# An expert loop of one expert per round, with the next expert's transposes ahead of the down product and single buffers for gathered rows and results

## The chip, the core and the metric

The program runs on one core of one Trainium2 chip. Its metric is the device time of one execution in microseconds (us). The kernel before was run three times; the median counts. One more execution was recorded by the hardware profiler.

## What is computed

Two layers of a hybrid backbone over 128 context and 512 latent tokens of width 1024, all in fp32. The change touches the last part of each layer, the expert-choice mixture: each of 16 experts picks the tokens with the highest affinity to it (16 context and 64 latent ones, 80 in all), runs them through its own SwiGLU network, and adds the weighted result to the residual.

```
aff = softmax(h @ w_router)
gsel, idx = lax.top_k(aff.transpose(0, 2, 1), C)        # C = 2*T/16: 16 or 64 tokens
xs = h[idx]                                             # each expert's tokens
hid = silu(xs @ w_gate[e]) * (xs @ w_up[e])
ye = hid @ w_down[e] * gsel
y = zeros.at[idx].add(ye);   x = x + g2 * y
```

Here h is the RMS-normed residual, modulated: h = norm(x) * (1 + scale) + shift.

## The kernel before

The kernel is written by hand for the five queues of the core (PE, DVE, ACT, POOL, SP), with counting semaphores; no scheduler reorders anything. A `Signal` holds a semaphore and how often it is raised per layer, and `at(l, n)` is the value after its n-th event of layer l. Each layer is unrolled in the program; only the expert loop is a loop of the hardware (`Fori`), on PE, DVE, ACT and SP. On POOL it is unrolled.

Per expert the work is as follows.

- **Weights.** SP copies w_gate, w_up and w_down of each expert in six units of 2 MB into the six slots of `weight_ring` (L345). Units 0 to 3 are the halves of gate and up, alternating; 4 and 5 are the halves of down. A slot is loaded again as soon as PE has raised `expert_used` for its last use.
- **Gather.** POOL fetches the 80 normed rows of an expert from DRAM (`x_unit`) by an indirect DMA into `picked` (`gather`, L1386), which has two buffers.
- **Transposes.** PE transposes the 80 x 1024 rows in eight pieces into PSUM banks 6 and 7 (`picked_transposes`, L695).
- **Modulation.** DVE multiplies them by the scale and adds the shift (`modulate_picked`, L1265 and L1267) into `picked_t`, which has two buffers, too.
- **Gate and up.** PE computes both with the weights as the stationary operand (`gate_up`, L708): 64 matmuls per unit in the source, 128 in execution, since the chip runs an fp32 matmul as two. ACT takes SiLU of the gate half (L924), DVE multiplies by the up half (`gated_hidden`, L1273).
- **Down.** PE computes 80 x 1024 results into banks 4 and 5 (`down`, L722), 16 matmuls in the source and 32 in execution.
- **Result.** DVE scales by the affinity and the gate (`gated_result`, L1280) into `added` (two buffers), and POOL adds it to `x_res` in DRAM by an indirect DMA that accumulates (L1407). Before each such scatter POOL waits for the one before, since two experts may pick the same token.

The PE loop runs eight rounds of two experts. In a round the even expert's transposes come first, then its gate and up; the odd expert's transposes stand ahead of the even expert's down product. The next round begins with the branch back (L727). DVE's loop has the same two-expert form.

```
with pe.Fori(0, EXPERTS // 2) as r:
    picked_transposes(r * 2, 0, r)
    gate_up(r * 2, 0)
    picked_transposes(r * 2 + 1, 1, r)
    down(r * 2)
    gate_up(r * 2 + 1, 1)
    down(r * 2 + 1)
```

Of the kernel before, what the change touches and what calls it, by code (L numbers as in the profile page):

```python
# [67 lines left out]
def build(nc, x_prompt, x_sample, c, cache_k, cache_v, c_ctx, norm1_g, w_mod, b_mod, w_in, conv_w, conv_b,  # L68
# [9 lines left out]
    with ctx:  # L78
# [20 lines left out]
        picked = qk_flat[0:CAP, 0:2 * D].rearrange("p (b n) -> p b n", b=2)  # L99
        added = qk_flat[0:CAP, 2 * D:4 * D].rearrange("p (b n) -> p b n", b=2)  # L100
# [3 lines left out]
        picked_t = v_sb[:, D:D + 2 * KD * CAP].rearrange("p (b k n) -> p b k n", b=2, k=KD)  # L104
# [146 lines left out]
        residual_written = [signal(f"residual_written{b}", 3 - b + EXPERTS // 2, 16) for b in range(2)]  # L251
# [15 lines left out]
        gathered = [signal(f"gathered{b}", EXPERTS // 2, 16) for b in range(2)]  # L267
        picked_transposed = signal("picked_transposed", EXPERTS)
        picked_scaled = signal("picked_scaled", EXPERTS)
        picked_ready = signal("picked_ready", EXPERTS)  # L270
# [22 lines left out]
        def tokens(t):  # L293
            return slice(t * P, (t + 1) * P)
# [107 lines left out]
        def _(pe):  # L402
# [64 lines left out]
            for l in range(DEPTH):  # L467
# [224 lines left out]
                def picked_transposes(e, b, rnd):  # L692
                    pe.wait_ge(*gathered[b].at(l, rnd + 1))
                    for k in range(KD):
                        last = nc.tensor.transpose(ps[:, 6 + k // 4, (k % 4) * CAP:(k % 4 + 1) * CAP],  # L695
                                                   picked[:, b, tokens(k)], ident[0:CAP, 0:CAP])
                    last.then_inc(picked_transposed.sem, 1)

                def gate_up(e, b):
                    pe.wait_ge(*picked_ready.at(l, e + 1))  # L700
                    for i in range(4):
                        pe.wait_ge(*expert_loaded[i].at(l, e + 1))
                        w = ring[:, UNIT_SLOTS[l][i], :].rearrange("p (k n) -> p k n", k=KD)
                        for f in range(BLK):
                            for k in range(KD):
                                for c in range(2):
# [3 lines left out]
                                        picked_t[:, b, k, :], start=(k == 0), stop=(k == KD - 1))  # L710
# [16 lines left out]
                with pe.Fori(0, EXPERTS // 2) as r:  # L727
                    picked_transposes(r * 2, 0, r)
                    gate_up(r * 2, 0)
                    picked_transposes(r * 2 + 1, 1, r)  # L730
                    down(r * 2)
                    gate_up(r * 2 + 1, 1)
                    down(r * 2 + 1)
# [209 lines left out]
        def _(dve):  # L943
# [39 lines left out]
            for l in range(DEPTH):  # L983
# [275 lines left out]
                def modulate_picked(e, b):  # L1259
                    dve.wait_ge(*picked_transposed.at(l, e + 1))  # L1260
                    dst = picked_t[:, b].rearrange("p (a k) n -> p a k n", a=2)
# [15 lines left out]
                def gated_result(e, b, rnd):  # L1277
                    dve.wait_ge(*expert_used.at(l, e * 6 + 6))
                    dve.wait_ge(*residual_written[b].at(l, rnd + (3 - b)))
                    nc.vector.scalar_tensor_tensor(added[:, b, :], ps[0:CAP, 4:6, :].rearrange("p b n -> p (b n)"),  # L1280
# [3 lines left out]
                with dve.Fori(0, EXPERTS // 2) as r:  # L1284
                    modulate_picked(r * 2, 0)
                    gated_hidden(r * 2)
                    modulate_picked(r * 2 + 1, 1)
                    gated_result(r * 2, 0, r)
                    gated_hidden(r * 2 + 1)
                    gated_result(r * 2 + 1, 1, r)  # L1290
# [14 lines left out]
        def _(pool):  # L1305
# [39 lines left out]
            for l in range(DEPTH):  # L1345
# [36 lines left out]
                def gather(e):  # L1382
                    b = e % 2
                    if e >= 2:
                        pool.wait_ge(*picked_transposed.at(l, e - 1))
                    nc.gpsimd.indirect_dma_start(  # L1386
                        out=picked[:, b, :], out_offset=None, in_=x_unit,
                        in_offset=bass.IndirectOffsetOnAxis(ap=row_idx[:, e:e + 1], axis=0))\
                      .then_inc(gathered[b].sem, 16)
# [4 lines left out]
                gather(1)  # L1394
# [5 lines left out]
                pool.wait_ge(*residual_written[0].at(l, 3))  # L1400
                pool.wait_ge(*residual_written[1].at(l, 2))
                for e in range(EXPERTS):
                    b = e % 2
                    if e > 0:
# [55 lines left out]
```

## Time and profile before

| | |
|---|---|
| median of 3 runs | 2212.54 us (2212.06 to 2217.48) |
| the profiled execution | 2215.38 us |
| its span, first to last instruction | 2213.3 us |
| mean granted TensorE clock | 0.941 of full |
| instructions | 45747 |
| expert loop of layer 0 | 481 to 1114 us |
| expert loop of layer 1 | 1572 to 2184 us |

The profile is of one execution. A busy time is the sum of an engine's instructions; PE is the matmuls, PEld the weight loads, which overlap them. An idle time stands with what ended it ("releaser"); "issue" means that the engine waited for nothing that the profile shows. [...] The two loops' ends are those of their last results.

### The profile page before, as it was taken

Reading aid. Unit: us, or ns where it says so; the run is one execution under the profiler, and the core shown is the slowest. Engines: PE = TensorE matmul, PEld = TensorE weight load, DVE = VectorE, ACT = ScalarE, POOL = GpSimd, SP = SyncE. Lnnn points to the kernel's source line nnn. Section 1 sums busy time; section 2 is a strip of 40 time slices with the busy share of each in tenths; the row PEclk is TensorE's granted clock in tenths of the full one; section 3 lists DMA queues with packets and bytes.
Section 4 is the critical chain, followed back from the end, with each engine's and each line's share of the span. In section 5 each row is a group of like instructions: output and inputs, shape, how many; then the busy total and the mean of one; then the engine's idle time right before and its main releaser. Section 6 shows DMA issues by size and latency. Waiting matters only on the chain.

```text
span 2213.3 us, 45747 instructions
## 1 busy us (share of the span) xinstructions
PE 1863.8 (84%) x21107; PEld 1234.8 (56%) x21107; DVE 634.5 (29%) x1040; ACT 310.5 (14%) x616; POOL 127.5 (6%) x155
## 2 busy tenths in 40 slices
PE   4999878959888898888859996888588888898884
PEld 2555455546665665656635553654456665766662
DVE  2089484250100110011020995823300101011011
ACT  3111253210000000000021113522000000000001
POOL 2000000100000000000010000000000000000000
PEclk9999989969999999999979998989799999999997
DMA  9247500539999999999731633033599999999993
GB/s 348 81 152 252 219 14 4 190 129 363 316 344 339 326 344 334 332 333 343 277 129 42 225 133 124 1 114 149 182 340 345 346 359 350 333 349 350 342 339 106
DMA packets 219937, 536.57 MB, mean 242 GB/s; under 512 B 5905, under 2 KB 6322, under 8 KB 219730
## 3 DMA queue, kind: packets, MB, share of 16 engines
q1 hardware_dynamic: 204416, 482.37, 60.6%
q0 software_dynamic: 12128, 41.82, 6.5%
q10 hardware_dynamic: 3186, 9.12, 1.0%
q8 instruction: 191, 3.13, 0.6%
q14 instruction: 16, 0.13, 0.0%
HBM read 508.64 MB, written 24.64 MB: 241 GB/s over the span
## 4 chain that ended last, share of the span: by engine, by line
PE 80%; DVE 8%; issue 7%; DMA 3%; ACT 2%; POOL 0%; DVEq 0%; ACTq 0%; POOLq 0%
PE ps L708 28%; PE ps L722 20%; PE ps L491 13%; PE ps L621 6%; PE ps L503 3%; PE ps L435 2%; DVE neg_m L1114 2%; PE ps L578 1%; PE ps L641 1%; PE ps L444 1%; DMA weight_ring<-in_conv_w_dram 1%; DMA out_dram<-conv_tmp 1%; DVE weight_ring L1150 1%; DVE v_sb L1267 1%; PE ps L695 1%
## 5 line engine op out<-in xcount | busy, mean ns | idle before, releaser
L708 PE MATMUL ps<-v_sb,weight_ring 128*64 128x80 f32 x16384 | 629.2, 241 | 150.5 <-issue 108.4
L708 PEld LDWEIGHTS ps<-v_sb,weight_ring 128*64 128x64 f32 x16384 | 611.5, 143 | 178.5 <-issue 177.6
L722 PE MATMUL ps<-weight_ring,mix 128*80 128x512 f32 x1024 | 445.7, 593 | 0.0
L722 PEld LDWEIGHTS ps<-weight_ring,mix 128*80 128x80 f32 x1024 | 151.0, 150 | 269.5 <-issue 268.0
L491 PE MATMUL ps<-mix,weight_ring 128*128 128x128 f32 (+1 forms) x1024 | 281.1, 435 | 4.9 <-DVE mix L1014 2.7
L491 PEld LDWEIGHTS ps<-mix,weight_ring 128*128 128x128 f32 x1024 | 155.7, 191 | 139.6 <-issue 134.2
L1273 DVE TENSOR_TENSOR mix<-mix,ps 128x320 f32<-128x320 f32 x64 | 31.2, 488 | 703.1 <-PE ps L708 703.1
L1044 DVE SCALAR_TENSOR_TENSOR weight_ring<-u_gate,conv_cols,weight_ring 128x655 f32<-128x655 f32 x240 | 195.1, 892 | 0.0
L924 ACT ACTIVATE mix<-ps 128x320 f32<-128x320 f32 x64 | 28.0, 438 | 1162.8 <-PE ps L708 1162.8
L1280 DVE SCALAR_TENSOR_TENSOR qk<-ps,gsel,gate 80x1024 f32<-80x1024 f32 x32 | 41.0, 1280 | 412.0 <-PE ps L722 412.0
L621 PE MATMUL ps<-weight_ring,mix 128*128 128x512 f32 x320 | 144.6, 608 | 1.9 <-issue 1.9
L1407 POOL DMA_INDIRECT x_res<-qk,row_idx x32 | 45.9, 1435 | 1173.0 <-DVE qk L1280 1102.4
L621 PEld LDWEIGHTS ps<-weight_ring,mix 128*128 128x128 f32 x320 | 61.3, 196 | 74.1 <-issue 74.1
L503 PE MATMUL ps<-weight_ring,mix 128*128 128x512 f32 x160 | 70.5, 596 | 0.0
L846 ACT ACTIVATE weight_ring<-ps,neg_m 128x640 f32<-128x640 f32 (+1 forms) x80 | 55.8, 706 | 2.1 <-DVE neg_m L1114 2.1
L1114 DVE TENSOR_REDUCE neg_m<-ps 128x2 f32<-128x1280 f32 (+1 forms) x40 | 50.8, 1274 | 16.6 <-PE ps L553 16.2
L503 PEld LDWEIGHTS ps<-weight_ring,mix 128*128 128x128 f32 x160 | 29.8, 190 | 40.0 <-issue 40.0
L564 PE MATMUL ps<-ident,weight_ring 128*128 128x128 f32 x168 | 32.9, 300 | 20.5 <-DVE o_tok L1133 10.0
L578 PE MATMUL ps<-v_sb,weight_ring 128*128 128x128 f32 x272 | 45.2, 310 | 4.8 <-ACT weight_ring L864 4.8
L435 PE MATMUL ps<-weight_ring,cond_silu 128*32 128x512 f32 x384 | 47.9, 617 | 0.8 <-issue 0.8
L1026 DVE TENSOR_TENSOR u_gate<-u_gate,conv_tmp 128x128 f32<-128x128 f32 (+1 forms) x16 | 7.2, 489 | 135.7 <-ACT conv_tmp L797 135.7
L578 PEld LDWEIGHTS ps<-v_sb,weight_ring 128*128 128x128 f32 x272 | 37.0, 208 | 11.1 <-ACT weight_ring L864 6.4
(176 smaller groups left out, 1146.2 us busy)
## 6 DMA issues: line engine op xcount, KB each, us to landing
weight_ring<-in_w_gate_dram SPq DMA_DIRECT2D x64, 2048.0 KB, 11.0
weight_ring<-in_w_up_dram SPq DMA_DIRECT2D x64, 2048.0 KB, 10.7
weight_ring<-in_w_down_dram SPq DMA_DIRECT2D x64, 2048.0 KB, 9.7
weight_ring<-in_w_mod_dram SPq DMA_DIRECT2D x24, 2048.0 KB, 8.2
weight_ring<-in_w_in_dram SPq DMA_DIRECT2D x10, 2048.0 KB, 12.1
weight_ring<-in_w_out_dram SPq DMA_DIRECT2D x4, 2048.0 KB, 10.5
x_res<-x_tile POOLq DMA_DIRECT2D x10, 512.0 KB, 3.7
x_unit<-x_norm ACTq DMA_DIRECT2D x10, 512.0 KB, 2.6
```

What stands on the lines that cost most here:

```text
L435: last = nc.tensor.matmul(ps[c * STRIP:(c + 1) * STRIP, 6, :], cond_silu[:, k, :], w[:, k, :], start=(k < 4), stop=(k >= 4))
L491: last = nc.tensor.matmul(ps[:, 2 * (n % 3) + bank, 0:cols.stop - cols.start], w[:, k, tokens(b)], mix[:, k, cols], start=(k == 0), stop=( ...
L503: last = nc.tensor.matmul(ps[:, 2 * (n % 3), :], mix[:, k, tokens(t)], w[:, k, :], start=(k == 0), stop=(k == KD - 1))
L578: last = nc.tensor.matmul(ps[:, 7, tokens(1)], a_col[:, tokens(j)], vals, start=(j == 0), stop=(j == n - 1))
L621: last = nc.tensor.matmul(ps[:, 2 * (i % 2) + n, :], mix[:, k, tokens(t)], w[:, k % 4, n * BANK:(n + 1) * BANK], start=(k == 0), stop=(k = ...
L708: last = nc.tensor.matmul(ps[c * HALF:(c + 1) * HALF, i, f * CAP:(f + 1) * CAP], w[:, k, o:o + HALF], picked_t[:, b, k, :], start=(k == 0) ...
L722: last = nc.tensor.matmul(ps[0:CAP, 4 + n, :], hid[:, k, :], w[:, kk, n * BANK:(n + 1) * BANK], start=(k == 0), stop=(k == KD - 1))
L846: last = nc.scalar.activation(prob[:, b, m, 0:n], score_rows(s)[:, m, :], ACT.Exp, bias=neg_m[:, b, m:m + 1], accum_out=row_sum[:, b, m:m ...
L1044: ins = nc.vector.scalar_tensor_tensor(acc[:, j, :], src, w, acc[:, j, :], ALU.mult, ALU.add)
L1114: nc.vector.tensor_reduce(neg_m[:, s % 2, :], score_rows(s), AX, ALU.max, negate=True)\
L1280: nc.vector.scalar_tensor_tensor(added[:, b, :], ps[0:CAP, 4:6, :].rearrange("p b n -> p (b n)"), gsel[:, bass.ds(e, 1)], gate2[:], ALU.mu ...
L1407: nc.gpsimd.indirect_dma_start(out=x_res, out_offset=bass.IndirectOffsetOnAxis(ap=row_idx[:, e:e + 1], axis=0), in_=added[:, b, :], in_off ...
```

## The change

PE's loop now runs 16 rounds of one expert: gate and up of e, transposes of e+1, down of e. The transposes of expert 0 stand ahead of the loop, and after the last expert a seventeenth set of rows is gathered, transposed and modulated, and not used. DVE's loop follows: hidden product of e, modulation of e+1, result of e. `picked`, `picked_t` and `added` have one buffer each. POOL gathers rows e+2 once the transposes of e+1 have read the buffer, and DVE writes a result once the scatter of the one before has landed. SP and ACT are unchanged.

```diff
--- before.py
+++ after.py
@@ -96,12 +96,12 @@
-        picked = qk_flat[0:CAP, 0:2 * D].rearrange("p (b n) -> p b n", b=2)
-        added = qk_flat[0:CAP, 2 * D:4 * D].rearrange("p (b n) -> p b n", b=2)
+        picked = qk_flat[0:CAP, 0:D]
+        added = qk_flat[0:CAP, 2 * D:3 * D]
...
-        picked_t = v_sb[:, D:D + 2 * KD * CAP].rearrange("p (b k n) -> p b k n", b=2, k=KD)
+        picked_t = v_sb[:, D:D + KD * CAP].rearrange("p (k n) -> p k n", k=KD)
@@ -248,7 +248,7 @@
-        residual_written = [signal(f"residual_written{b}", 3 - b + EXPERTS // 2, 16) for b in range(2)]
+        residual_written = [signal("residual_written0", 3 + EXPERTS, 16), signal("residual_written1", 2, 16)]
@@ -264,10 +264,10 @@
-        gathered = [signal(f"gathered{b}", EXPERTS // 2, 16) for b in range(2)]
-        picked_transposed = signal("picked_transposed", EXPERTS)
-        picked_scaled = signal("picked_scaled", EXPERTS)
-        picked_ready = signal("picked_ready", EXPERTS)
+        gathered = signal("gathered", EXPERTS + 1, 16)
+        picked_transposed = signal("picked_transposed", EXPERTS + 1)
+        picked_scaled = signal("picked_scaled", EXPERTS + 1)
+        picked_ready = signal("picked_ready", EXPERTS + 1)
@@ -689,14 +689,14 @@
-                def picked_transposes(e, b, rnd):
-                    pe.wait_ge(*gathered[b].at(l, rnd + 1))
+                def picked_transposes(e):
+                    pe.wait_ge(*gathered.at(l, e + 1))
...
                         last = nc.tensor.transpose(ps[:, 6 + k // 4, (k % 4) * CAP:(k % 4 + 1) * CAP],
-                                                   picked[:, b, tokens(k)], ident[0:CAP, 0:CAP])
+                                                   picked[:, tokens(k)], ident[0:CAP, 0:CAP])
...
-                def gate_up(e, b):
+                def gate_up(e):
                     pe.wait_ge(*picked_ready.at(l, e + 1))
                     for i in range(4):
                         pe.wait_ge(*expert_loaded[i].at(l, e + 1))
@@ -707,7 +707,7 @@
-                                        picked_t[:, b, k, :], start=(k == 0), stop=(k == KD - 1))
+                                        picked_t[:, k, :], start=(k == 0), stop=(k == KD - 1))
@@ -724,13 +724,11 @@
-                with pe.Fori(0, EXPERTS // 2) as r:
-                    picked_transposes(r * 2, 0, r)
-                    gate_up(r * 2, 0)
-                    picked_transposes(r * 2 + 1, 1, r)
-                    down(r * 2)
-                    gate_up(r * 2 + 1, 1)
-                    down(r * 2 + 1)
+                picked_transposes(0)
+                with pe.Fori(0, EXPERTS) as e:
+                    gate_up(e)
+                    picked_transposes(e + 1)
+                    down(e)
@@ -1256,9 +1254,9 @@
-                def modulate_picked(e, b):
+                def modulate_picked(e):
                     dve.wait_ge(*picked_transposed.at(l, e + 1))
-                    dst = picked_t[:, b].rearrange("p (a k) n -> p a k n", a=2)
+                    dst = picked_t.rearrange("p (a k) n -> p a k n", a=2)
@@ -1274,20 +1272,18 @@
-                def gated_result(e, b, rnd):
+                def gated_result(e):
                     dve.wait_ge(*expert_used.at(l, e * 6 + 6))
-                    dve.wait_ge(*residual_written[b].at(l, rnd + (3 - b)))
-                    nc.vector.scalar_tensor_tensor(added[:, b, :], ps[0:CAP, 4:6, :].rearrange("p b n -> p (b n)"),
+                    dve.wait_ge(*residual_written[0].at(l, e + 3))
+                    nc.vector.scalar_tensor_tensor(added, ps[0:CAP, 4:6, :].rearrange("p b n -> p (b n)"),
                                                    gsel[:, bass.ds(e, 1)], gate2[:], ALU.mult, ALU.mult)\
                       .then_inc(result_taken.sem, 1)
...
-                with dve.Fori(0, EXPERTS // 2) as r:
-                    modulate_picked(r * 2, 0)
-                    gated_hidden(r * 2)
-                    modulate_picked(r * 2 + 1, 1)
-                    gated_result(r * 2, 0, r)
-                    gated_hidden(r * 2 + 1)
-                    gated_result(r * 2 + 1, 1, r)
+                modulate_picked(0)
+                with dve.Fori(0, EXPERTS) as e:
+                    gated_hidden(e)
+                    modulate_picked(e + 1)
+                    gated_result(e)
@@ -1380,38 +1376,35 @@
                 def gather(e):
-                    b = e % 2
-                    if e >= 2:
-                        pool.wait_ge(*picked_transposed.at(l, e - 1))
+
+                    if e > 0:
+                        pool.wait_ge(*picked_transposed.at(l, e))
+                    at = e % EXPERTS
                     nc.gpsimd.indirect_dma_start(
-                        out=picked[:, b, :], out_offset=None, in_=x_unit,
-                        in_offset=bass.IndirectOffsetOnAxis(ap=row_idx[:, e:e + 1], axis=0))\
-                      .then_inc(gathered[b].sem, 16)
+                        out=picked, out_offset=None, in_=x_unit,
+                        in_offset=bass.IndirectOffsetOnAxis(ap=row_idx[:, at:at + 1], axis=0))\
+                      .then_inc(gathered.sem, 16)
...
                 pool.wait_ge(*result_taken.at(l, 1))
                 pool.wait_ge(*unit_stored.at(l, TILES))
                 gather(0)
-                gather(1)
                 if l == DEPTH - 1:
...
-                pool.wait_ge(*residual_written[0].at(l, 3))
+                gather(1)
                 pool.wait_ge(*residual_written[1].at(l, 2))
                 for e in range(EXPERTS):
-                    b = e % 2
-                    if e > 0:
-                        pool.wait_ge(*residual_written[1 - b].at(l, 2 + b + (e + 1) // 2))
+                    pool.wait_ge(*residual_written[0].at(l, 3 + e))
                     pool.wait_ge(*result_taken.at(l, e + 2))
                     nc.gpsimd.indirect_dma_start(
                         out=x_res, out_offset=bass.IndirectOffsetOnAxis(ap=row_idx[:, e:e + 1], axis=0),
-                        in_=added[:, b, :], in_offset=None, compute_op=ALU.add)\
-                      .then_inc(residual_written[b].sem, 16)
-                    if e + 2 < EXPERTS:
+                        in_=added, in_offset=None, compute_op=ALU.add)\
+                      .then_inc(residual_written[0].sem, 16)
+                    if e + 2 <= EXPERTS:
                         gather(e + 2)
-                pool.wait_ge(*residual_written[1].at(l, 2 + EXPERTS // 2))
-                pool.wait_ge(*residual_written[0].at(l, 3 + EXPERTS // 2))
+                pool.wait_ge(*residual_written[0].at(l, 3 + EXPERTS))
```

In the built program the PE queue around the loop reads as follows. A row x256 are 256 matmuls of the source; in execution each is two matmuls and two weight loads, a transpose is one of each. Before, from the entry of the loop (`v_sb` holds `picked_t`, `qk` the gathered rows, `mix` the hidden product):

```order
L727 UNCONDITIONAL_BRANCH
L727 ISA
L695 MATMUL ps<-ident,qk 128x80 x8
L700 ISA
L702 REGISTER_ALU
L708 MATMUL ps<-v_sb,weight_ring 64x80 x256
L695 MATMUL ps<-ident,qk 128x80 x8
L717 ISA
L722 MATMUL ps<-weight_ring,mix 80x512 x8
L717 REGISTER_ALU
L722 MATMUL ps<-weight_ring,mix 80x512 x8
...
L727 COMPARE_AND_BRANCH
```

Here the first transposes stand behind the branch of each round, and the body holds two sets of every product.

The same place after the change:

```order
L695 MATMUL ps<-ident,qk 128x80 x8
L728 UNCONDITIONAL_BRANCH
L728 ISA
L702 REGISTER_ALU
L708 MATMUL ps<-v_sb,weight_ring 64x80 x256
L693 ISA
L695 MATMUL ps<-ident,qk 128x80 x8
L717 ISA
L722 MATMUL ps<-weight_ring,mix 80x512 x8
L717 REGISTER_ALU
L722 MATMUL ps<-weight_ring,mix 80x512 x8
...
L728 COMPARE_AND_BRANCH
```

The first transposes have moved ahead of the loop's entry, the body holds one expert, its first matmuls are those of gate and up, and the branch back follows each down product.

On DVE's queue, from the entry of its loop to the branch back (`ps` is PSUM). Before:

```order
L1284 UNCONDITIONAL_BRANCH
...
L1265 TENSOR_TENSOR v_sb<-ps,scale_x 128x640
L1267 TENSOR_TENSOR v_sb<-v_sb,shift_x 128x640
...
L1273 TENSOR_TENSOR mix<-mix,ps 128x320
...
L1265 TENSOR_TENSOR v_sb<-ps,scale_x 128x640
L1267 TENSOR_TENSOR v_sb<-v_sb,shift_x 128x640
...
L1280 SCALAR_TENSOR_TENSOR qk<-ps,gsel,gate 80x1024
...
L1284 COMPARE_AND_BRANCH
```

The modulation stands first in a round, ahead of the hidden product. After:

```order
L1263 TENSOR_TENSOR v_sb<-ps,scale_x 128x640
L1265 TENSOR_TENSOR v_sb<-v_sb,shift_x 128x640
L1283 UNCONDITIONAL_BRANCH
...
L1271 TENSOR_TENSOR mix<-mix,ps 128x320
...
L1271 TENSOR_TENSOR mix<-mix,ps 128x320
...
L1263 TENSOR_TENSOR v_sb<-ps,scale_x 128x640
L1265 TENSOR_TENSOR v_sb<-v_sb,shift_x 128x640
...
L1278 SCALAR_TENSOR_TENSOR qk<-ps,gsel,gate 80x1024
...
L1283 COMPARE_AND_BRANCH
```

The modulation (a product, then a sum into `v_sb`) of the next expert now stands between the hidden product and the result of every expert.

## Rows read from the trace of the kernel before

**Rows 1.** The page: busy time, share of the span and instructions of PE.

```profile
PE 1863.8 (84%) x21107; PEld 1234.8 (56%) x21107; DVE 634.5 (29%) x1040; ACT 310.5 (14%) x616; POOL 127.5 (6%) x155
```

**Rows 2.** The page: the chain that ended last, by engine and line.

```profile
PE ps L708 28%; PE ps L722 20%; PE ps L491 13%; PE ps L621 6%; PE ps L503 3%; PE ps L435 2%; DVE neg_m L1114 2%; PE ps L578 1%; PE ps L641 1%; PE ps L444 1%; DMA weight_ring<-in_conv_w_dram 1%; DMA out_dram<-conv_tmp 1%; DVE weight_ring L1150 1%; DVE v_sb L1267 1%; PE ps L695 1%
```

**Rows 3.** Waits of PE, whole span: us in total, times, longest.

```profile
PE ps L708 <- issue: 108.4, 69, 2.9
PE ps L708 <- DVE v_sb L1267: 42.0, 16, 2.8
```

**Rows 4.** Timeline of PE, one pair of layer 0: start, us, what [idle before].

```profile
717.93 0.72 PE L695 MATMUL ps<-ident,qk 80*128 80x80 f32 x8
721.38 11.65 PE L708 MATMUL ps<-v_sb,weight_ring 128*64 128x80 f32 x278 [2.73 <-DVE v_sb L1267]
734.85 4.65 PE L708 MATMUL ps<-v_sb,weight_ring 128*64 128x80 f32 x128 [1.82 <-issue]
740.77 3.90 PE L708 MATMUL ps<-v_sb,weight_ring 128*64 128x80 f32 x106 [1.27 <-issue]
...
759.04 8.38 PE L708 MATMUL ps<-v_sb,weight_ring 128*64 128x80 f32 x236
767.86 4.65 PE L708 MATMUL ps<-v_sb,weight_ring 128*64 128x80 f32 x128 [0.44 <-issue]
774.88 7.12 PE L708 MATMUL ps<-v_sb,weight_ring 128*64 128x80 f32 x148 [2.37 <-issue]
781.93 13.96 PE L722 MATMUL ps<-weight_ring,mix 128*80 128x512 f32 x32
```

**Rows 5.** The same of layer 1.

```profile
1727.52 13.89 PE L708 MATMUL ps<-v_sb,weight_ring 128*64 128x80 f32 x338 [2.73 <-DVE v_sb L1267]
...
1777.30 4.65 PE L708 MATMUL ps<-v_sb,weight_ring 128*64 128x80 f32 x128 [1.74 <-issue]
1783.51 3.26 PE L708 MATMUL ps<-v_sb,weight_ring 128*64 128x80 f32 x88 [1.57 <-issue]
1786.70 13.96 PE L722 MATMUL ps<-weight_ring,mix 128*80 128x512 f32 x32
```

**Rows 6.** The page: DMA queues, the one of instructions (packets, MB, share).

```profile
q8 instruction: 191, 3.13, 0.6%
```

**Rows 7.** DMA queues, 558 to 1034 us, then 1648 to 2107 us: six pairs each.

```profile
q8 instruction: 65, 1.06, 0.9%
...
DMA packets 64790, 159.18 MB, mean 347 GB/s; under 512 B 1535, under 2 KB 1535, under 8 KB 64730
...
q8 instruction: 60, 0.98, 0.9%
```

**Rows 8.** Line 727: the branch (min/median/max ns, first and last start).

```profile
L727 PEldq COMPARE_BRANCH  x6: 4281/4796/5424, 630.6 to 1027.3; - x6
...
L727 PEldq COMPARE_BRANCH  x1: 5416/5416/5416, 788.2 to 788.2; - x1
...
L727 PEldq COMPARE_BRANCH  x7: 6221/6255/6305, 1640.2 to 2100.2; - x7
```

**Rows 9.** Groups by line: second step of the modulation (busy us, mean ns | idle).

```profile
L1267 DVE TENSOR_TENSOR v_sb<-v_sb,shift_x 128x640 f32<-128x640 f32 x32 | 27.1, 848 | 1.1
```

**Rows 10.** Windows: PE busy (count), PEld, DVE, ACT, POOL, granted clock, DMA share, GB/s.

```profile
722.00:723.00 1.00, 1.00 (x20) 1.00 (x18) 0.00 (x0) 0.00 (x0) 0.87 (x1) 0.50 1.04 422
736.00:737.00 1.00, 1.00 (x36) 1.00 (x34) 0.00 (x0) 0.00 (x0) 0.00 (x0) 1.00 1.04 403
```

**Rows 11.** DMA issues: gather and scatter, us from issue to landing.

```profile
qk<-x_unit,row_idx POOLq DMA_INDIRECT x32, 8.5
x_res<-qk,row_idx POOLq DMA_INDIRECT x32, 8.3
```

**Rows 12.** Waits of PE, 558 to 1034 us, then 1648 to 2107 us.

```profile
PE ps L708 <- issue: 47.2, 28, 2.9
...
PE ps L708 <- issue: 39.4, 27, 2.1
```

## The prediction

> **What bounds the kernel now.** The page comes first: PE is busy 84% of the span [rows 1], and the chain that ended last runs 28% through the gate/up matmuls (L708) and 20% through the down matmuls (L722) [rows 2]. So the expert loop is read on PE. The list of waits then says what PE lacks there: 42.0 us in 16 waits for DVE's modulation of the gathered tokens (L1267), and 108.4 us in 69 stops marked "issue", for which the profile names no partner [rows 3]. The first is what the change aims at; the second has to be understood before it can be priced.
>
> The PE timeline of one pair of layer 0 [rows 4] shows both. An even expert opens with its eight transposes, waits 2.73 us for DVE, then runs gate/up. The odd one has had its transposes ahead of the even expert's down product and starts without a wait. The "issue" stops stand 128 matmuls apart, but not where a weight unit (128 executed matmuls) ends: 278 = 2x128 + 22, and in the odd expert 236 = 2x128 - 20. In layer 1 they stand 82 behind a unit's end (338 = 2x128 + 82) [rows 5]. A late weight transfer would stop PE at a unit's first matmul, so this is no weight wait. 128 matmuls with their loads are 256 instructions, and the "instruction" queue moved 3.13 MB in 191 packets, 16.4 KB each, 64 bytes for each of 256 instructions [rows 6]. **PE waits for its own program**, one block at a time. A block is consumed in 4.65 us, and the next arrives 4.65 plus the stop after the last one was entered: 5.9 and 7.0 us in layer 0, 6.2 in layer 1 [rows 4, 5]. Only the block ahead is held: after a down product (32 matmuls, 13.9 us) PE meets one boundary freely, then stops again. Meanwhile the weights keep the DMA engines at 347 GB/s in layer 1 [rows 7], and a block of program has to pass between them.
>
> The loop's branch tells the rest. It costs the queue 4.3 to 5.4 us in layer 0 and 6.2 to 6.3 in layer 1 each time it is taken [rows 8]: the loop's first block is fetched again. It starts 6.2 to 6.3 us after the down product does (781.93 and 788.2) [rows 4, 8], because PE's queue runs ahead, so 13.9 us of matmuls cover it. Today there is one such branch per two experts.
>
> [...]
>
> **The change part by part.** (1) The wait. Every expert's transposes now stand ahead of the previous down product. DVE's two steps, the second 0.85 us [rows 9], were inside the 2.73 us and now lie beside 13.9 us. Fourteen waits of 2.73 us go, 38 us, and with them the slower clock behind them: at 722 us the granted clock is 0.50 and 20 matmuls run in a microsecond, at 736 it is 1.00 and 36 run [rows 10]; at 128 in 4.65 us the even expert's first 278 would take 10.1, and they take 11.65, 1.6 us more [rows 4].
>
> (2) The single buffers. The gather for e+2 is issued after the scatter of e, about 2 us behind e's down product, and lands in 8.5 us; it is wanted 23 us or more after that product ended. A scatter lands in 8.3 us, its buffer is wanted an expert later (38 us). Both are covered, cost 0; were a cover gone, its price would be the landing time less the distance, nothing until the distance falls below about 12 us [rows 11]. POOL waits for the previous scatter before each scatter as before. A wait of DVE for the scatter holds back only its next step, the product with the SiLU, at least two units (9.3 us) behind. One transposition too many per layer: 2 x 0.7 = 1.4 us.
>
> (3) The branch, taken for every expert: 30 times instead of 14. This is the term that decides. Counted in the built program, the body falls from 2221 PE instructions to 1112 (272 matmuls of four instructions, eight transposes of two, eight others). Where blocks end in it follows from today's stops. Layer 0: the body starts 17 instructions later (hoisted transposes and their wait), so today's boundary 64 instructions in (16 of them transposes) is now 47 in, again 22 matmuls into gate/up. The body then spans 47 + 4x256 + 41: six blocks, and the one fetched ahead before the branch makes seven fetches per expert; today 65 packets in 12 experts, 5.4 [rows 7]. Layer 1: the body starts 1075 = 4x256 + 51 instructions earlier, so the boundary moves from 184 to 235: 235 + 3x256 + 109, five blocks, six fetches; today 60 in 12, or 5.
>
> Now one expert from the start D of a down product. **Layer 0:** branch at 6.2, median duration 4.8 [rows 8], first block there at 11.0. The second block is fetched only then. No row of before shows that fetch bare, since the wait for DVE covers it; the nearest rows are the branches, 4.3 to 6.3 us, and I take 5.4, near their middle: 16.4. The last block is entered late (13 matmuls inside the down product), so the block fetched beyond it is still under way at the branch, 0 to 1.1 us; I take 1.1: 17.5. Gate/up starts at 13.9 and needs that block after 22 matmuls, at 14.7: a **new stop of 2.8 us**. Three blocks at 6.5 us, between the mean over all stops (4.65 + 47.2/28 = 6.3) and the 7.0 seen [rows 4, 12]: 37.0. Then 106 matmuls 3.9 and transposes 0.7: the next D at **41.6 us**. Today's pairs take (1027.3 - 630.6)/5 = 79.3 us [rows 8], 39.65 per expert: +1.95, times 15 = +29 us. A halved clock behind the new stop costs nothing more: 4.65 + 1.6 stays under 6.5.
>
> **Layer 1:** 6.2 + 6.25 + 5.4 = 17.9; PE gets there after 116 matmuls, at 18.1, so it hardly stops. Three blocks at 6.2 (the mean with every stop is 4.65 + 39.4/27 = 6.1 [rows 12]): 36.7; 12 matmuls and the transposes 1.15: **37.85** against (2100.2 - 1640.2)/12 = 38.35: -0.5, times 15 = -7.5 us. The waits removed were mostly time in which the store refilled; the refill remains.
>
> Sum: 29 - 7.5 + 1.4 = +23 us. The profiled execution took 2215.4 us for a span of 2213.3, the median of the runs is 2212.5; against that, **2235 us**. Bounds: layer 0 at its cheapest is 6.2 + 4.8 + 4.3 + 3x6.3 + 4.6 = 38.8 (-13 us), at its dearest 6.2 + 5.4 + 6.3 + 1.1 + 3x7.0 + 4.6 = 44.6 (+74); layer 1 37.5 to 39.4 (-12 to +16). All ends at once (2189, 2304) is unlikely; two thirds of the way on either side gives 2204 and 2281, and I take **2204 to 2278**.
>
> **Rivals.**
> - *The wait goes and nothing takes its place* (0.06). The branch has been hidden so far, 6.3 us used of 13.9. Then 38.5 us are saved, 2174, or 2152 with the clock (14 x 1.6). Against it: the stop-to-stop times are set by fetches, and a fetch needs 6 us wherever the wait stood.
> - *Six fetches in both layers* (0.09), if the boundary in layer 0 falls over 88 instructions into the body, as when something ahead of it counts otherwise than I count. Layer 0 then takes about 38.2 as well, 1.45 less per expert: -22 - 7.5 + 1.4, 2184. This is the point at which the sign turns.
> - *The forecast* (0.60), and *layer 0 near its dear end* (0.10), 2275, DMA queues as full as now and the stop at every boundary nearer 7.
>
> Hence faster 0.19, same 0.11, slower 0.70.
>
> **What would show it.** The instruction queue's packets rise from 191 to about 231 (+24 in layer 0, +16 in layer 1). The branch row shows 32, 30 of them 4 to 6.5 us. No wait for L1267 beyond the first of each layer. In layer 0 a stop of 2 to 4 us stands 22 matmuls behind each down product, and experts 41 to 42 us apart; in layer 1 the stops stand at 116, 244, 372 and experts 38 us apart. Branches of under 0.1 us, a packet count below 200, or stops at unit ends would prove the reasoning wrong; layer 0 under 39.5 us per expert would make the forecast wrong.

## The result

The changed kernel takes **2071.2 us** (median of 4 runs, 2065.4 to 2074.0) against 2215.0 before (2212.1 to 2221.4): a ratio of 0.934, 95% interval 0.931 to 0.937. It is 144 us faster, where 2235 and a range from 2204 were forecast.

### The profile after

The page, first its part 1 for PE, then the queue of instructions and the chain that ended last (shares of the span by engine, then by line); they answer to [rows 1, 2, 6].

```profile
PE 1832.2 (89%) x21123; PEld 1203.2 (58%) x21123; DVE 638.6 (31%) x1044; ACT 310.4 (15%) x616; POOL 129.3 (6%) x157
...
q8 instruction: 36, 0.59, 0.1%
...
PE 66%; DMA 23%; DVE 8%; ACT 1%; issue 1%; POOL 0%; ACTq 0%; DVEq 0%; POOLq 0%
DMA weight_ring<-in_w_up_dram 20%; PE ps L708 16%; PE ps L722 15%; PE ps L491 14%; PE ps L621 7%; PE ps L503 3%; PE ps L435 2%; DVE neg_m L1112 2%; PE ps L695 1%; PE ps L444 1%; PE ps L641 1%; PE ps L578 1%; DMA weight_ring<-in_conv_w_dram 
```

The instruction queue moved 36 packets, not the 231 of the forecast and not the 191 of before. A new partner stands first in the chain: the transfer of w_up into the weight ring, 20% of the span.

The branch of PE's loop (line 728 now; min/median/max ns, first and last start), against [rows 8]:

```profile
L728 PEldq COMPARE_BRANCH  x32: 76/208/246, 522.4 to 2031.6; - x32
```

Thirty taken branches cost about 0.2 us each; before they cost 4.3 to 6.3. Nothing is fetched for them: between 530 and 1040 us, fifteen rounds of layer 0, the instruction queue moved no packet.

The longest waits of PE (us in total, times, longest), against [rows 3]:

```profile
PE ps L708 <- DMA weight_ring<-in_w_up_dram: 30.3, 18, 1.9
...
PE ps L708 <- DVE v_sb L1265: 3.9, 2, 1.9
PE ps L708 <- issue: 2.9, 3, 1.6
```

Of the 42.0 us for the modulation 3.9 are left, the first wait of each layer, and of the 108.4 us of "issue" 2.9; 30.3 us for weights have come. The three "issue" stops stand in the first round of each layer, in which the loop's blocks still come. The gate and up of that round, first in layer 0, then in layer 1, up to its first stop:

```profile
495.26 16.41 PE L708 MATMUL ps<-v_sb,weight_ring 128*64 128x80 f32 x406 [1.93 <-DVE v_sb L1265]
...
1495.56 15.07 PE L708 MATMUL ps<-v_sb,weight_ring 128*64 128x80 f32 x372 [1.92 <-DVE v_sb L1265]
```

406 is 3 x 128 + 22 and 372 is 2 x 128 + 116: the blocks end where the prediction had counted, 22 and 116 matmuls in. From the second round on there is no such stop.

The counts behind this, in instructions per product, stand in the trace too (count, then min/median/max ns, first and last start):

```profile
L708 PEld LDWEIGHTS ps<-v_sb,weight_ring x16384: 132/137/232, 495.2 to 2024.5; 128*64 128x64 f32 x200
L708 PE MATMUL ps<-v_sb,weight_ring x16384: 229/233/393, 495.3 to 2024.5; 128*64 128x80 f32 x200
...
L695 PEld LDWEIGHTS ps<-ident,qk x272: 137/141/230, 492.0 to 2025.2; 80*128 80x128 f32 x136
L695 PE MATMUL ps<-ident,qk x272: 232/233/366, 492.0 to 2025.2; 80*128 80x80 f32 x136
...
L722 PEld LDWEIGHTS ps<-weight_ring,mix x1024: 146/150/152, 516.2 to 2038.4; 128*80 128x80 f32 x171
L722 PE MATMUL ps<-weight_ring,mix x1024: 591/592/652, 516.3 to 2038.8; 128*80 128x512 f32 x171
```

The source has 256 fp32 matmuls of gate and up and 16 of down for each of 32 experts, 8192 and 512. They ran as 16384 and 1024 matmuls with as many weight loads: four instructions each. The 272 transposes (8 x 17 x 2 layers) ran as 272 and 272: two each. So 1104 of the body's 1112 instructions are these; the other eight are waits, register steps and the branch of the built program.

The timeline of PE (start, us, what, idle before) shows when, for an early and a late expert of layer 0, against [rows 4]:

```profile
562.39 18.08 PE L708 MATMUL ps<-v_sb,weight_ring 128*64 128x80 f32 x512
580.40 0.77 PE L695 MATMUL ps<-ident,qk 80*128 80x80 f32 x8
581.01 13.90 PE L722 MATMUL ps<-weight_ring,mix 128*80 128x512 f32 x32
...
862.90 13.66 PE L708 MATMUL ps<-v_sb,weight_ring 128*64 128x80 f32 x384
878.40 4.65 PE L708 MATMUL ps<-v_sb,weight_ring 128*64 128x80 f32 x128 [1.84 <-DMA weight_ring<-in_w_up_dram]
882.98 0.77 PE L695 MATMUL ps<-ident,qk 80*128 80x80 f32 x8
883.70 13.96 PE L722 MATMUL ps<-weight_ring,mix 128*80 128x512 f32 x32
897.59 13.75 PE L708 MATMUL ps<-v_sb,weight_ring 128*64 128x80 f32 x384
```

The early expert runs 512 matmuls of gate and up without a stop; the next gate/up starts 32.5 us later (562.39 to 594.84). The late one stops once, 384 matmuls in, which is the end of a weight unit, and takes 34.7 us (862.90 to 897.59). The granted clock is 1.00 between 558 and 1023 us, and the DMA engines have no pause (columns as in [rows 10]):

```profile
558.00:1023.00 465.00, 449.74 (x7709) 322.57 (x7708) 53.47 (x69) 28.92 (x41) 32.77 (x28) 1.00 1.04 381
```

So the loop has a new bound. At its start all six units lie in the ring, and PE, with 32.5 us, uses them up faster than they come; after some seven experts the stock is gone and the transfers set 34.7 us. From the branches, the mean expert of layer 0 takes (1028.7 - 522.4)/15 = 33.75 us for 39.65 before, in layer 1 33.75 for 38.35: 88 + 69 = 157 us. The span fell by 143.8. Most of the rest is the start of layer 0's loop, at 492.0 us for 481.5; it moves from run to run, since in e5 to e7 below, whose code and loads ahead of the loop are those of before, it stood at 490.8, 484.8 and 495.1.

### The profile page after: what moved, and what is told of

Its sections match the earlier page's. It is cut to its first block, busy times and chain, and to the rows that moved or that the text cites. A ratio compares the mean times of both kernels' runs of the same rounds, so it can differ in the third digit from the quotient of the medians.

```text
span 2069.5 us, 45859 instructions
## 1 busy us (share of the span) xinstructions
PE 1832.2 (89%) x21123; PEld 1203.2 (58%) x21123; DVE 638.6 (31%) x1044; ACT 310.4 (15%) x616; POOL 129.3 (6%) x157
## 2 busy tenths in 40 slices
DMA packets 219974, 534.68 MB, mean 258 GB/s; under 512 B 5937, under 2 KB 6354, under 8 KB 219922
## 4 chain that ended last, share of the span: by engine, by line
PE 66%; DMA 23%; DVE 8%; ACT 1%; issue 1%; POOL 0%; ACTq 0%; DVEq 0%; POOLq 0%
DMA weight_ring<-in_w_up_dram 20%; PE ps L708 16%; PE ps L722 15%; PE ps L491 14%; PE ps L621 7%; PE ps L503 3%; PE ps L435 2%; DVE neg_m L1112 2%; PE ps L695 1%; PE ps L444 1%; PE ps L641 1%; PE ps L578 1%; DMA weight_ring<-in_conv_w_dram 1%; DMA out_dram<-conv_tmp 1%; DVE weight_ring L1148 1%
## 5 line engine op out<-in xcount | busy, mean ns | idle before, releaser
L708 PE MATMUL ps<-v_sb,weight_ring 128*64 128x80 f32 x16384 | 588.6, 234 | 37.2 <-DMA weight_ring<-in_w_up_dram 30.3
L708 PEld LDWEIGHTS ps<-v_sb,weight_ring 128*64 128x64 f32 x16384 | 578.0, 138 | 67.0 <-DMA weight_ring<-in_w_up_dram 33.2
L1112 DVE TENSOR_REDUCE neg_m<-ps 128x2 f32<-128x1280 f32 (+1 forms) x40 | 50.8, 1274 | 16.8 <-PE ps L553 16.4
L564 PE MATMUL ps<-ident,weight_ring 128*128 128x128 f32 x168 | 32.5, 297 | 20.4 <-DVE o_tok L1131 10.0
L1171 DVE TENSOR_TENSOR conv_tmp<-ps,u_gate 128x1024 f32<-128x1024 f32 x10 | 12.2, 1225 | 104.5 <-PE ps L621 104.5
```

The source lines that it names most:

```text
L708: last = nc.tensor.matmul(ps[c * HALF:(c + 1) * HALF, i, f * CAP:(f + 1) * CAP], w[:, k, o:o + HALF], picked_t[:, k, :], start=(k == 0), s ...
L1112: nc.vector.tensor_reduce(neg_m[:, s % 2, :], score_rows(s), AX, ALU.max, negate=True)\
```

## The experiments

Two theories. **S:** PE's store keeps the blocks of a loop that is short enough and fetches a long one again in each round; the change made the body short (1112 instructions for 2221). **W:** the gain is the removed wait, with the clock behind it, as the change's order of work suggests.

### e1: the long body back

```diff
-                with pe.Fori(0, EXPERTS) as e:
-                    gate_up(e)
-                    picked_transposes(e + 1)
-                    down(e)
+                with pe.Fori(0, EXPERTS // 2) as r:
+                    gate_up(r * 2)
+                    picked_transposes(r * 2 + 1)
+                    down(r * 2)
+                    gate_up(r * 2 + 1)
+                    picked_transposes(r * 2 + 2)
+                    down(r * 2 + 1)
```

> The changed kernel with PE's loop alone written as 8 rounds of two experts in the same order of work (body of 2216 PE instructions for 1112); DVE, POOL, buffers and every product stay. Theory S (PE keeps a short loop in its store and fetches a long one again in every round): the branch row goes back to 4 to 6.5 us, the instruction queue to about 190 packets for 36, stops stand 128 matmuls apart, no wait for the modulation comes back; 2180 to 2215 us. Theory W (the gain is the removed wait and the clock behind it, the body's length is nothing): branch and time as in the changed kernel, 2071 us.

Measured: 2206.3 us against 2215.8 of before, ratio 0.996 (0.994 to 0.999). Its branch, its instruction queue and PE's longest wait, each from its own view, then a stretch of its timeline:

```profile
L728 PEldq COMPARE_BRANCH  x16: 76/5064/6300, 558.0 to 2169.6; - x16
...
q8 instruction: 199, 3.26, 0.6%
...
PE ps L708 <- issue: 144.6, 91, 2.7
```

```profile
643.90 1.04 PE L708 MATMUL ps<-v_sb,weight_ring 128*64 128x80 f32 x22
646.66 4.65 PE L708 MATMUL ps<-v_sb,weight_ring 128*64 128x80 f32 x128 [1.72 <-issue]
653.41 6.29 PE L708 MATMUL ps<-v_sb,weight_ring 128*64 128x80 f32 x128 [2.10 <-issue]
660.15 4.65 PE L708 MATMUL ps<-v_sb,weight_ring 128*64 128x80 f32 x128 [0.45 <-issue]
666.62 3.90 PE L708 MATMUL ps<-v_sb,weight_ring 128*64 128x80 f32 x106 [1.82 <-issue]
```

S holds, W falls. The order of work is that of the changed kernel, no wait for the modulation is left beyond the first of each layer, and yet only some 10 us of the 144 are gained. This kernel and the changed one differ in nothing but the form of PE's loop, so **the length of the body alone is worth 135 us** (2206.3 against 2071.2). The stop that the prediction had placed behind a bare branch is there: 22 matmuls into gate and up (643.90), 1.72 us, where it had 2 to 4. Where the wait stood, the fetch now shows: "issue" rose from 108.4 to 144.6 us while nearly all of the 42.0 us of waits went.

### e2: the wait back, the body short

```diff
-                picked_transposes(0)
                 with pe.Fori(0, EXPERTS) as e:
+                    picked_transposes(e)
                     gate_up(e)
-                    picked_transposes(e + 1)
                     down(e)
```

DVE's loop follows (modulation, hidden product, result), and the seventeenth gather is left out.

> One expert per round, but the transposes of e stand at the head of its own round, so PE waits for the modulation in every round (16 per layer for 8 before the change). Theory S: the body of about 1113 instructions stays in the store, 36 packets, branch 0.2 us; an expert costs 32.5 + 2.7 + 0.2 and up to 1.6 for the clock, 35.4 to 37.0 for 33.75: 2120 to 2170 us, still faster than before the change. Theory W: twice the waits of before, so slower than before by about 65 us, 2280.

Measured: 2131.9 us, ratio 0.963 (0.959 to 0.968). The branch, the instruction queue and the wait, each from its own view, then two experts of the timeline:

```profile
L727 PEldq COMPARE_BRANCH  x32: 76/208/238, 521.9 to 2092.5; - x32
...
q8 instruction: 36, 0.59, 0.1%
...
PE ps L708 <- DVE v_sb L1264: 83.0, 32, 2.7
```

```profile
641.20 17.93 PE L708 MATMUL ps<-v_sb,weight_ring 128*64 128x80 f32 x512 [2.65 <-DVE v_sb L1264]
...
676.23 19.57 PE L708 MATMUL ps<-v_sb,weight_ring 128*64 128x80 f32 x512 [2.65 <-DVE v_sb L1264]
```

The short body stays in the store again. With 32 waits in place of 16, the kernel is 84 us faster than before. It pays 83.0 us of waits, and every second expert runs its first matmuls at the lower clock (512 matmuls in 19.57 us for 17.93; the granted clock is 0.70 from 677 to 678 us). From here to the changed kernel it is 61 us: that is what taking away all 32 waits is worth **when the body is short**, about 1.9 us for each. Under a long body (e1 against before) 16 waits went and 10 us came of it, about 0.6 us for each.

### e5, e6, e7: how long a body stays

The kernel before, its two-expert rounds shortened by leaving blocks of the contraction out of gate and up (here for 6 of 8):

```diff
-                            for k in range(KD):
+                            for k in range(6):
...
-                                        picked_t[:, b, k, :], start=(k == 0), stop=(k == KD - 1))
+                                        picked_t[:, b, k, :], start=(k == 0), stop=(k == 5))
```

> The kernel before (two experts per round) with gate and up contracted over 7 of 8 blocks of 128; the eighth is left out of the computation, its weights are still loaded. The body falls from 2221 to 1965 PE instructions. Counted from the stops of before, it touches 9 blocks of 256 in layer 0 and 8 in layer 1. What a short loop needs is not known: if PE's store holds 8 blocks, the branch of layer 0 stays at 4 to 6.5 us and that of layer 1 falls to about 0.2 us, unless the block fetched ahead takes one of the eight, in which case both stay long. If it holds 7 or fewer, both stay long too. The instruction queue's packets tell the same: about 10 fewer than before per resident round.

> The same with 6 of 8 blocks contracted (two left out of the computation): a body of 1709 instructions, 8 blocks in layer 0 and 7 in layer 1. With a store of 8 blocks that includes the one ahead, layer 1 is resident (branch 0.2 us) and layer 0 is not; with 8 blocks besides, both are; with 7 or fewer and one ahead, neither.

> The same with 5 of 8 blocks contracted (three left out of the computation): 1453 instructions, 7 blocks in layer 0 and 6 in layer 1. With a store of 8 blocks both are resident in either reading; only a store of 7 with one ahead would leave layer 0 with long branches. The changed kernel's 6 blocks in layer 0 are known to stay.

The branch row of e5 (whole span), of e6 in layer 0 and in layer 1, and of e7 (whole span), each followed by what its instruction queue moved:

For e5:

```profile
L727 PEldq COMPARE_BRANCH  x16: 83/6245/6312, 553.9 to 2080.9; - x16
...
q8 instruction: 175, 2.87, 0.6%
```

For e6:

```profile
L727 PEldq COMPARE_BRANCH  x8: 83/6180/6277, 542.0 to 1030.6; - x8
...
L727 PEldq COMPARE_BRANCH  x8: 83/215/253, 1550.9 to 2028.7; - x8
...
q8 instruction: 103, 1.69, 0.3%
```

For e7:

```profile
L727 PEldq COMPARE_BRANCH  x16: 83/215/242, 546.7 to 2024.3; - x16
...
q8 instruction: 38, 0.62, 0.1%
```

e6 is the telling one: the same 1709 instructions are fetched again in each round of layer 0 (6.2 us a branch) and stay in layer 1 (0.2 us). By the count of the prediction the body touches 8 blocks of 256 in layer 0 (64 + 6 x 256 + 109 instructions) and 7 in layer 1 (184 + 5 x 256 + 245). The first round of e6 bears the count out; its gate and up, first in layer 0, then in layer 1, up to the first stop:

```profile
488.01 12.01 PE L708 MATMUL ps<-v_sb,weight_ring 128*64 128x80 f32 x278 [1.86 <-DVE v_sb L1267]
...
1498.58 13.98 PE L708 MATMUL ps<-v_sb,weight_ring 128*64 128x80 f32 x338 [1.86 <-DVE v_sb L1267]
```

278 and 338 are 22 and 82 matmuls behind a unit's end, as in [rows 4, 5]. e5 with 9 and 8 blocks stays in neither layer, e7 with 7 and 6 in both. In these runs **a loop that touched 7 blocks or fewer stayed** (0.2 us a branch), and one that touched 8 did not (6.2 us). There was no half: e6's body in layer 0, one block too long, was fetched again whole. Between its first and its last branch there, seven rounds, the instruction queue moved:

```profile
q8 instruction: 62, 1.02, 0.8%
```

That is about 9 packets for each round, the eight blocks and the one ahead. In layer 1, between 1551 and 2028.7 us, it moved none. Whether the block ahead takes an eighth place in the same store or is held apart from the seven, no run tells.

The times (2121.1, 2068.5 and 2064.4 us) are not comparable, since work is left out.

### e8: the fetch under light traffic

In the kernel before, half of every weight unit is loaded and used twice:

```diff
-                kk = KD if i < 4 else KD // 2
-                sp.dma_start(ring[:, UNIT_SLOTS[l][i], :]...
+                kk = KD // 2 if i < 4 else KD // 4
+                sp.dma_start(ring[:, UNIT_SLOTS[l][i], 0:UNIT // 2]...
...
-                                        ps[...], w[:, k, o:o + HALF],
+                                        ps[...], w[:, k % 4, o:o + HALF],
```

The sources of the transfers and the down product are halved alike.

> The kernel before (two experts per round) with half of each weight unit loaded and used twice; the other half is left out of the computation. PE's instructions stay, 191 packets of program as before. If a fetch takes 6 us because it waits behind weight packets (DMA 0.96 busy), then with half the weights it takes under 4.65 us mostly, the issue stops shrink from 108 us to under 40 and the branches to 2 to 4 us: 2212 - 70 to 100, 2110 to 2140 us. If the 6 us are the fetch's own latency, nothing changes: 2205 to 2215.

Measured: 2115.6 us, ratio 0.956 (0.952 to 0.960). Its branch, and the stops for the program:

```profile
L727 PEldq COMPARE_BRANCH  x16: 83/3406/3830, 558.2 to 2090.2; - x16
...
PE ps L708 <- issue: 32.2, 24, 3.0
```

A good part of the fetch's length is queueing behind weights: with 197 GB/s between 558 and 1034 us for 335, branches of 3.3 to 3.8 us for 4.3 to 6.3, 24 stops for 69. How long a fetch takes with no other traffic, no run shows. The reading of the "issue" stops as fetches that share the DMA engines was right.

### e3: the changed kernel without its new bound

The same edit in the changed kernel.

> The changed kernel with half of each weight unit loaded (1 MB for 2 MB) and each half used twice in the products; the other half of the expert weights is left out of the computation. PE's instructions stay. Theory S with weights as the new bound of the second half of each loop: the waits for w_up (30 us) go, every expert takes the 32.5 us of its matmuls, 2071 - 30 x 1.25 = about 2034 us. If PE itself or the fetch is what remains, 2071.

Measured: 2023.1 us, ratio 0.914 (0.910 to 0.918), 48 us under the changed kernel. In the window view PE is busy in all of 400 us:

```profile
560.00:960.00 400.00, 400.00 (x6990) 288.80 (x6988) 47.33 (x61) 27.64 (x39) 30.38 (x26) 1.00 0.70 217
```

Every expert takes 32.3 us. This is the floor of PE's own work in this form. The expected 2034 was 11 us too high: it counted the waits for w_up alone, and the matmuls of gate and up got shorter, too (578.4 us busy for 588.6).

### e4, e9: longer runs in DRAM

The transfers of gate and up read 2 KB at a time, those of down 4 KB; over the span the changed kernel moved its 534.68 MB in 219974 packets, e4 the same in 154438. The edit makes the former like the latter, and PE accumulates over two units:

```diff
-                    return w[l, e].rearrange("(k p) n -> p k n", p=P)[:, :, (i // 2) * BANK:(i // 2 + 1) * BANK]
+                    return w[l, e].rearrange("(k p) n -> p k n", p=P)[:, (i // 2) * 4:(i // 2) * 4 + 4, :]
...
-                        for f in range(BLK):
-                            for k in range(KD):
+                        for f in range(2 * BLK):
+                            bank, at = 2 * (f // BLK) + i % 2, f % BLK * CAP
+                            for kk in range(KD // 2):
+                                k = i // 2 * (KD // 2) + kk
```

A bank's accumulation now begins with its first block alone (start at k == 0 and f % BLK == 0), ACT waits for unit 2 and DVE for unit 3 for both halves.

> The changed kernel with gate and up loaded as w_down is, in units of 4 x 128 rows of the full 1024 columns, so that each run in DRAM is 4 KB for 2 KB; the products accumulate over two units, and SiLU and the hidden product of both halves follow units 2 and 3. In the changed kernel packets of 4 KB took 164 ns and those of 2 KB 90 ns in the stretch that waits for weights. If that is the price per byte, an expert's weights come in about 33 us for 34.7, PE with 32.5 nearly binds, and the time is 2035 to 2050 us. If the rate is set elsewhere, 2071. If the later SiLU and product hold up the down product, slower than 2071 by up to 1 us per expert, 2100.

> The kernel of e4 once more, beside e10 on the same chip: 2037 us, within 0.3%.

Measured: 2037.3 us, ratio 0.921 (0.917 to 0.924), and again 2039.8, ratio 0.920 (0.917 to 0.923). A late expert of e4, and its window view:

```profile
886.37 13.50 PE L710 MATMUL ps<-v_sb,weight_ring 128*64 128x80 f32 x384
900.73 4.65 PE L710 MATMUL ps<-v_sb,weight_ring 128*64 128x80 f32 x128 [0.86 <-DMA weight_ring<-in_w_up_dram]
...
919.96 13.50 PE L710 MATMUL ps<-v_sb,weight_ring 128*64 128x80 f32 x384
```

```profile
880.00:1010.00 130.00, 126.43 (x2198) 90.99 (x2197) 14.90 (x20) 6.91 (x11) 9.37 (x8) 1.00 1.03 393
```

From 558 to 1023 us it is 393 GB/s, too, for the 381 of the changed kernel; a late expert takes 33.6 us for 34.7, and in layer 0 the stock lasts for eleven experts in place of seven. **This version beats both kernels**, by 8% against before and by some 33 us against the change. It did not run side by side with the changed kernel, but each ran beside the kernel before, and the intervals of the ratios lie apart (0.917 to 0.924 and 0.931 to 0.937).

### e10: longer runs still

```diff
-                return w_down[l, e].rearrange("(k p) n -> p k n", p=P)[:, (i - 4) * 4:(i - 3) * 4, :]
+                return w_down[l, e].rearrange("(p k) n -> p k n", p=P)[:, (i - 4) * 4:(i - 3) * 4, :]
...
-                                    o = f * P + c * HALF
+                                    o = c * HALF * KD + f
-                                        ps[...], w[:, kk, o:o + HALF],
+                                        ps[...], w[:, kk, o:o + (HALF - 1) * KD + 1:KD],
```

> The kernel of e4 with w_down's rows laid so that a partition takes four neighbouring rows, 16 KB in one run of DRAM; the hidden index of partition m in block f becomes 8m + f, so gate and up take every eighth column of their weights as the stationary operand. If longer runs still help and strided weight loads cost nothing, the last 1.1 us per expert of waits for w_up go: 2023 to 2032 us. If runs of 4 KB are already at the transfers' full rate, 2037. If a weight load with a stride of 32 bytes is slower than its matmul (138 ns now, started every 36), every expert gets longer, well over 2100 us.

Measured: 2452.4 us, ratio 1.106 (1.103 to 1.109). The groups of gate/up in e10 and, under it, in e4 (busy us, mean ns | idle before):

```profile
L710 PE MATMUL ps<-v_sb,weight_ring 128*64 128x80 f32 x16384 | 1001.4, 285 | 3.9 <-DVE v_sb L1268 3.9
L710 PEld LDWEIGHTS ps<-v_sb,weight_ring 128*64 128x64 f32 x16384 | 996.6, 218 | 28.3 <-issue 28.3
```

```profile
L710 PE MATMUL ps<-v_sb,weight_ring 128*64 128x80 f32 x16384 | 581.3, 234 | 12.6 <-DMA weight_ring<-in_w_up_dram 7.2 <-DVE v_sb L1268 3.9 <-issue 1.5
L710 PEld LDWEIGHTS ps<-v_sb,weight_ring 128*64 128x64 f32 x16384 | 574.4, 138 | 38.8 <-issue 30.3 <-DMA weight_ring<-in_w_up_dram 8.4
```

A weight load that takes every eighth column lasts 218 ns for 138, and PE's gate and up grow from 581.3 to 1001.4 us. The third case of the expectation; whether runs over 4 KB help the transfers stays open, since PE became far slower than they are: between 560 and 1100 us it was busy throughout, at a DMA share of 0.79 and 288 GB/s.

## Why the prediction was wrong

- **What bounds the kernel: right.** The "issue" stops are PE waiting for its program, a block of 256 instructions at a time (stops 128 matmuls and their 128 loads apart, 191 packets of 16.4 KB), behind weight traffic (e8: traffic halved, stops from 108.4 to 32.2 us).
- **Part (1), the wait: right in kind.** It went, with the slower clock (between 558 and 1023 us 1.00; before, from 558 to 1034 us, 0.96). Its worth depended on what stood behind it: 10 us for 16 waits under a long body (e1), 61 us for 32 under a short one (e2). For a long body the prediction's words "the refill remains" hold, since "issue" grew by 36 us in e1. The first rival, which priced the wait alone at 2174 or 2152, had the right mechanism for a minor share.
- **Part (2), the single buffers: nothing seen.** No wait of PE for gathered rows beyond the first of each layer shows. The prediction wanted the rows 23 us or more after a down product ended; it was 18.1 (594.84 to 612.95), which still covers the 2 us and a landing of 7.6. A version with two buffers was not tried.
- **Part (3), the branch: the step that failed.** It said that the branch would be taken 30 times "instead of 14" and took it as given that each one fetches its target at 4.3 to 6.3 us, seven fetches per expert in layer 0 and six in layer 1, hence 41.6 and 37.85 us per expert. Measured are 0.2 us for the branch, no fetch at all after the first round, and 33.75 us per expert in both layers. The branch rows of before could not carry this: in all of them the target lay 8 or more blocks back. From stops at every boundary I had concluded that only the block ahead is held. The runs show two different things: PE fetches one block ahead (about 9 packets for the 8 blocks of each round in e6's layer 0), and it also keeps the blocks it has run, seven of them (0.2 us a branch in e6's layer 1 and in e7). A loop of six or five blocks was fetched once (36 packets in all) and then never again. The blocks counted per round, 6 and 5, were right, as the first rounds show, and with e5 to e7 they place the limit; but the price of some 6 us that each carried was not paid. Two of the prediction's own signs of an error came: a packet count below 200, and layer 0 under 39.5 us per expert.
- **The arithmetic for a loop that is fetched** stood up in the one case that was tested. In e1 the expert behind the bare branch took 41.0 us from one down product to the next (630.07 to 671.06), where the sum had 41.6. The stop 22 matmuls into gate and up was 1.72 us for the 2.8 of the sum, and the blocks behind it came every 6.5 to 6.8 us for 6.5. A loop that is fetched once per expert, as the forecast had it, was never measured.
- **The rival "the loop stays in PE's store"** was the truth, with a chance of 0.04 against "nothing but the size". It forecast 2108; 37 us of that were too much, because it put every expert at 35.5 us, near what the transfers need. In fact the first seven or so experts of each layer live on the six units already loaded and take PE's own 32.5 us.

The prediction had two things in hand: the sizes of the two bodies (2221 and 1112 instructions), on which its rival stood, and an observation (one block ahead) that did not speak about keeping at all. It let the second settle the question; no row of before could have, since no loop short enough to stay was in them.

## What to carry to other kernels

In this kernel the length of the loop's body decided more than the wait that the change was made for. Count the PE instructions of a hardware loop, and the blocks of 256 that they touch. In these traces 8704 fp32 matmuls of the source ran as 17408 matmuls and 17408 weight loads, four instructions each, and 272 transposes as 272 of each, two. With seven blocks or fewer the loop was fetched once (0.2 us a branch: the change, e2, e7, and e6 in layer 1); with eight or more it was fetched again in every round (6.2 us a branch: e5, and e6 in layer 0 with 62 packets in seven rounds). With 342 GB/s on the DMA engines (e1, 558 to 1034 us) the long body cost 135 us here (e1 against the change), more than the 42 us of waits that one would like to remove. Stops at a fixed distance of matmuls (128 here), at places that are not unit ends, were the sign (69 before, 91 in e1, 3 after the change); the packets of the instruction queue went with them (191, 199, 36). And when such stops go, look at the transfers next, since the run length in DRAM was worth another 1.5% here (e4, e9).

## What was unexpected of the hardware

- A store of PE that keeps a loop of up to 7 blocks of 256 instructions whole, and nothing of one of 8: branch 0.2 us and no packet against 6.2 us and about 9 packets a round, for a body of the same 1709 instructions in e6's two layers.
- Transfers in runs of 4 KB moved 393 GB/s; with two thirds of the weights in runs of 2 KB it was 381 GB/s, both without a pause of the DMA engines (shares 1.03 and 1.04 between 558 and 1023 us).
- A weight load of 64 columns at a stride of eight elements takes 218 ns for 138, and matmuls that were started every 35 ns (581.3 us over 16384) every 61.
